# Block 1 of a two-block model kernel: the matrix memory's keys scaled, and its values placed, by ScalarE's evictions instead of by VectorE

## The chip, the cores and the metric

The kernel runs on one core of one Trainium2 chip. The metric is the device time of one execution in microseconds (us), as the median of several runs. Inputs lie in HBM in float32; the program is one launch.

## The reference, cut to what matters

The program is two blocks one after the other, each of two layers. The change lies in the first block ("block 1"), which takes 256 tokens `x` and 256 context tokens `ctx` of width 1024. Each of its layers normalizes and modulates them, projects them to 3,344 columns, and runs three mixers on pieces of the projection: a gated MLP (a), an attention (b) and a matrix memory, mLSTM, in chunks of 128 tokens (c).

```python
(au, av, az, bq, bk, bv, bz, cq, ck, cv, co, cz, cg) = _split_proj(xn @ w_in)
...
qf = qc.astype(jnp.float32)
kf = kc.astype(jnp.float32) * (D ** -0.5)          # D = 64: the factor 0.125
vf = vc.astype(jnp.float32)
...
C_new = decay[..., None, None] * C + jnp.einsum('blh,blhd,blhe->bhde', wk, vf, kf)
n_new = decay[..., None] * n + jnp.einsum('blh,blhe->bhe', wk, kf)
...
s = jnp.einsum('bthd,bshd->btsh', qf, kf) * jnp.exp(dmat - m_t[:, :, None])
num = jnp.einsum('btsh,bshd->bthd', s, vf) + inter[..., None] * jnp.einsum('bhde,bthe->bthd', C, qf)
den = jnp.sum(s, axis=2) + inter * jnp.einsum('bhe,bthe->bth', n, qf)
```

So the keys `ck` are used only times 0.125, in products with the queries and with the weighted values. The values `cv` are used with a column of ones beside them, which gives the denominators in the same products.

## The kernel before, in words

All five engines run streams of their own, written out by hand, and are tied together by semaphores. The four tiles of 128 tokens are t = 0, 1 (context) and t = 2, 3 (latent). The projection is stored in `P` (128 partitions x 4 tiles x 3,344 columns); the names AU to CG on line 35 are the columns where its pieces begin (CK = 2304, CV = 2560, CO = 2816, BZ = 1536).

The projection is made in seven chunks of columns (`CHUNKS`, line 51), in this order; below they are "chunk 0" to "chunk 6". Chunk 4 is 2048 to 2560, the memory's queries and keys. Chunk 5 is 2560 to 3072, its values and its output gate. Chunk 6 is 1536 to 2048. In the second layer (l = 1) the context tiles need less: of chunk 4 only the keys, of chunk 5 only the values, of chunk 6 nothing (`CTX_LAST`, line 53).

- TensorE. In layer 0 `project_split` (L2532) takes each of the eight blocks k of the contracted width against all four tiles, with three matmuls for each tile (lines 2546 to 2548, of high and low parts that GpSimd makes on lines 1527 and 1536). A tile has its own PSUM bank 0 to 3, and the first matmul of a tile in a chunk waits until ScalarE has emptied that bank of the chunk before (L2544). In layer 1 `project` (L2522, matmuls on L2528) makes one tile after another, in banks taken in turn; a unit waits for the eviction of four units earlier. Between the chunks TensorE does small products for the modulation vectors (L2464 and L2477 in layer 0, L2452 in layer 1).
- ScalarE. It evicts each unit from PSUM to `P` with one activation (function `evict`, L1680 to L1684), counted on the semaphore `evict`, and after each chunk does that chunk's part of `post` (L1709): after chunk 5 a tanh of the gate columns, which waits in `from_dve` for VectorE's signal `d2a` (semaphore), since VectorE's stream decides when the scratch `E` is free.
- VectorE. In `block1` (L2217) it waits until a chunk's evictions are counted, then runs `post` (L2078). After chunk 5 that is lines 2092 to 2096: scale the keys of all four tiles by 0.125 in place, copy each tile's values from `P` to `VX`, set the column of ones beside them, and `silu_part` (L1983), whose memset (L1985) is the signal `d2a` and which then waits for the tanh and makes the sigmoid of it in place (L1852). Every instruction waits for the one before it (`link`). In layer 1 it also multiplies and adds modulation weights from the ring of DMA buffers (`ada_ops`, lines 1889 and 1891), a chunk of them after the post of chunk 5.
- `VX` has 4 tiles x 4 heads x 65 columns: 64 of values and a one. It is read by GpSimd (L1551, values times weights) and by TensorE (L2702), both after the last chunk. The scaled keys are read by TensorE: transposed (L2759) and in the products of line 2710. The columns of `P` that held the values are later scratch for a tanh (L1805).

All elementwise helpers of VectorE share their lines: `tt` is L1849, `ts` is L1852 or L1853.

Of the kernel before, what the change touches and what calls it, by code (L numbers as in the profile page):

```python
# [19 lines left out]
ACT = mybir.ActivationFunctionType  # L20
# [14 lines left out]
AU, AV, AZ, BQ, BK, BV, BZ, CQ, CK, CV, CO, CZ, CG = 0, 256, 512, 768, 1280, 1408, 1536, 2048, 2304, 2560, 2816, 3072, 3328  # L35
# [97 lines left out]
def build(nc, A, out):  # L133

    es = ExitStack()
    with es:
        def sb(name, cols, rows=128):
            return es.enter_context(nc.sbuf_tensor(name, [rows, cols], F32))[:, :]
# [9 lines left out]
        P = Pf.rearrange("p (t d) -> p t d", t=T)  # L148
# [46 lines left out]
        VX = sb("VX", 16 * 65).rearrange("p (t h n) -> p t h n", t=4, h=4)  # L195
# [15 lines left out]
        def bank(b, lo=0, hi=512):  # L211
            return ps[:, b * 512 + lo:b * 512 + hi]
# [33 lines left out]
        def S(name):  # L246
            if name not in sem:
                sem[name] = es.enter_context(nc.semaphore(name))
            return sem[name]
# [1231 lines left out]
        def mlstm_units(l):  # L1481

            return [(j, d) for j in range(4) for d in range(2) if j >= 2 or l == 0]
# [73 lines left out]
        def _(act):  # L1557
            c = Count()
            s_ = nc.scalar
# [5 lines left out]
            def b128(ap):  # L1565
                return ap.partition_broadcast(128)
# [73 lines left out]
            def norm(tiles, scale, shift, mods=0, dst=None):  # L1640

                normalized_rows(tiles)
                if mods:
                    act.wait_ge(S("mods_done"), mods)
                transposed_rows(tiles, scale, shift, dst)
# [15 lines left out]
            def first_layer_rows(scale, shift):  # L1661

                def high(k):
                    act.wait_ge(S("xt_act" if k % 2 == 0 else "xt_dve"), k // 2 + 1)
                    s_.activation(XH[:, k], XT[:, k], ACT.Copy).then_inc(S("xt_hi"), 1)

                first_rows()
                act.wait_ge(S("mods_done"), 1)
                transposed_block(0, range(T), scale, shift)
                transposed_block(2, range(T), scale, shift)  # L1670
                act.wait_ge(S("hk_out"), 16)
                high(0)
                high(1)
                for k in (2, 4, 6):
                    if k + 2 < KB:
                        transposed_block(k + 2, range(T), scale, shift)
                    high(k)
                    high(k + 1)

            def evict(dst, src):  # L1680

                u = c.up("evict") - 1
                act.wait_ge(S("proj"), u + 1)
                s_.activation(dst, src(bank(u % 4)), ACT.Copy).then_inc(S("evict"), 1)  # L1684

            def from_dve():
                act.wait_ge(S("d2a"), c.up("d2a"))

# [3 lines left out]
            def rstd_small(dst, src, n):  # L1692

                from_dve()
                s_.activation(dst, src, ACT.Sqrt, scale=1.0 / n, bias=eps).then_inc(S("a2d"), 1)
# [13 lines left out]
            def post(l, ci, L):  # L1709
                if ci == 0:  # L1710

                    from_dve()
                    link(s_.activation(BB[:, 0:32], BB[:, 0:32], ACT.Exp, scale=-1.0))
                    s_.activation(BB[:, 0:32], BB[:, 0:32], ACT.Ln, bias=ones[:, 0:1]).then_inc(S("a2d"), 1)
                    silu_part(CZ, CZ + 256, L, Ef)
                elif ci == 2:
                    rstd_small(hr, hs, HD)
                elif ci == 3:
                    silu_part(AZ, AZ + 256, L, Ef)
                    for t in range(0, len(L), 2):  # L1720
                        gelu_part(L[t:t + 2])
                elif ci == 4:
                    rstd_small(lnv, lnv, HD)
                elif ci == 5:
                    silu_part(CO, CO + 256, L, Ef)
# [53 lines left out]
            def block1(l):  # L1779
                L = list(range(T)) if l == 0 else list(LAT)  # L1780
                if l == 0:
                    act.wait_ge(S("const_in"), 16)
                if l == 0:
                    first_layer_rows(lambda s: A1[:, 0, s, :], lambda s: M1[:, 0, s, 0:8])
                else:
                    norm(range(T), lambda s: A1[:, l, s, :], lambda s: M1[:, l, s, 0:8], mods=l + 1)
                for k, (lo, hi) in enumerate(CHUNKS):
                    for t in range(T):
                        rng = (lo, hi) if (t >= 2 or l == 0) else CTX_LAST[k]
                        if rng:  # L1790
                            evict(P[:, t, rng[0]:rng[1]], lambda b, r=rng: b[:, 0:r[1] - r[0]])
                    if k < 6:
                        post(l, k, L)

                for a in range(4):
                    evict(QT[:, a, L[0] * 128:512], lambda b: b[:, L[0] * 128:512])
                for a in range(2):
                    evict(KT[:, a, :], lambda b: b)
                for m in (MQT, MKT):
                    for a in range(2):  # L1800
                        evict(m[:, a, L[0] * 128:512], lambda b: b[:, L[0] * 128:512])

                act.wait_ge(S("evict"), c.at("evict"))
                for half, w in enumerate((CQ, CV)):
                    s_.activation(P[:, L[0]:T, w:w + 256], P[:, L[0]:T, BZ + 256 * half:BZ + 256 * half + 256],  # L1805
                                  ACT.Tanh, scale=0.5).then_inc(S("bz_tanh"), 1)

                attention_block1(l, [(q, h) for q in range(8) if q % 4 >= 2 or l == 0 for h in range(4)])
                for n in range(len(mlstm_units(l))):
                    act.wait_ge(S("z_T"), 8 * l + n + 1)  # L1810
                    if n >= 2:
                        act.wait_ge(S("num"), 8 * l + n - 1)
                    s_.activation(E[:, n % 2, 0:512], bank(4 + n % 2), ACT.Copy).then_inc(S("z_T_sb"), 1)
                if l == 1:
                    act.dma_start(GF, b128(A["g_final"])).then_inc(S("gf_in"), 16)
                rstd_small(hs[:, 0:16], hs[:, 0:16], HD)
                gate_rows_out(2 if l == 0 else 1)
                for kb in (0, 1, 6, 7):
                    evict(XT[:, kb, L[0] * 128:512], lambda b: b[:, L[0] * 128:512])

            def gate_rows_out(n):
                for s in range(n):
                    act.wait_ge(S("gate_rows"), c.up("gate_rows"))
                    s_.activation(GR[:, s, :], ps[:, 2048 + 1024 * s:3072 + 1024 * s], ACT.Copy
                                  ).then_inc(S("gate_rows_sb"), 1)

            block1(0)
            block1(1)

            twice_normalized_rows()  # L1830
# [4 lines left out]
        def _(dve):  # L1835
            c = Count()
            v = nc.vector

            def link(ins):
                ins.then_inc(S("chain_dve"), 1)  # L1840
                dve.wait_ge(S("chain_dve"), c.up("chain_dve"))
# [9 lines left out]
            def ts(out_, a, s1, s2=None, op0=ALU.mult, op1=ALU.add):  # L1851
                return v.tensor_scalar(out_, a, s1, s2, op0, op1) if s2 is not None else \  # L1852
                    v.tensor_scalar(out_, a, s1, None, op0)  # L1853
# [224 lines left out]
            def post(l, ci, L):  # L2078
                if ci == 0:
                    gates(l)  # L2080
                    silu_part(CZ, CZ + 256, L, Ef)
                elif ci == 2:
                    qk_norm(l)
                elif ci == 3:
                    silu_part(AZ, AZ + 256, L, Ef)
                    for t in range(0, len(L), 2):
                        gelu_part(L[t:t + 2])
                elif ci == 4:
                    layer_norm_v(L)
                elif ci == 5:  # L2090

                    link(ts(P[:, :, CK:CV], P[:, :, CK:CV], 0.125))
                    for t in range(T):
                        link(v.tensor_copy(VX[:, t, :, 0:64], P[:, t, CV:CO].rearrange("p (h d) -> p h d", h=4)))
                        link(v.memset(VX[:, t, :, 64:65], 1.0))
                    silu_part(CO, CO + 256, L, Ef, sigmoid=True)

# [312 lines left out]
            for g in range(3):  # L2410
                dve.wait_ge(S("hk_ps"), g + 1)
                hi, lo = (Qf[0:48, (3 * a + g) * HANKEL:(3 * a + g + 1) * HANKEL] for a in range(2))
# [474 lines left out]
```

## Time and profile before

| | us |
|---|---|
| median of 3 runs | 1719.9 |
| lowest and highest of the 3 | 1708.89, 1721.32 |
| the profiled execution, device time | 1723.63 |
| its span, first to last instruction | 1721.8 |
| TensorE (PE) busy in it | 1559.4 (91%) |
| VectorE (DVE) busy | 1006.2 (58%) |
| ScalarE (ACT) busy | 682.6 (40%) |
| GpSimd (POOL) busy | 171.9 (10%) |

Times in rows are us from the start of the span. "L1684" is line 1684 of the kernel; "ps" is PSUM. A row of a timeline gives start, length, engine, line, operation, what is written and what is read, and in brackets how long the engine had been idle and which instruction ended the wait. Block 1's layer 0 projects from 50 to 215 us, layer 1 from 365 to 550 us.

### The profile page before, as it was taken

How to read it: one execution, taken by the hardware profiler on the slowest of the kernel's cores; microseconds unless marked ns; L12 is line 12 of the kernel's file. 1: busy time of each engine (PE TensorE's matmuls, PEld its weight loads, DVE VectorE, ACT ScalarE, POOL GpSimd, SP SyncE). 2: the span in 40 equal slices, each digit the busy share in tenths (PEclk: the TensorE clock that was granted, in tenths of full speed). 3: DMA queues.
4: the chain of work that ended last, by engine and by line, in shares of the span. 5: the costliest groups of instructions: out<-in, count | busy, mean ns of one | idle time of the engine just before them, and what ended most of it. 6: DMA issues, size and time to landing. Idle time of an engine off the chain costs nothing.

```text
span 1721.8 us, 19030 instructions
## 1 busy us (share of the span) xinstructions
PE 1559.4 (91%) x7325; PEld 1144.0 (66%) x7325; DVE 1006.2 (58%) x1575; ACT 682.6 (40%) x1083; POOL 171.9 (10%) x194
## 2 busy tenths in 40 slices
PE   5999977888999687999989998979999898979998
PEld 2777852655655363887778877557887776567886
DVE  2348365733384653776477755457776463257776
ACT  3302137212122423563036611136664665246663
POOL 1657520000000102000110010000000000000000
PEclk8999988889999768999899988989999898989999
DMA  9656502002567213775566653059886340068882
GB/s 343 214 164 243 176 20 97 28 1 98 181 224 258 70 61 113 217 256 173 147 185 232 226 151 111 0 183 305 294 296 219 122 147 1 0 208 290 300 302 98
DMA packets 186471, 290.70 MB, mean 169 GB/s; under 512 B 13739, under 2 KB 95115, under 8 KB 186380
## 3 DMA queue, kind: packets, MB, share of 16 engines
q1 hardware_dynamic: 172080, 273.56, 46.6%
q0 software_dynamic: 13200, 13.03, 3.4%
q10 hardware_dynamic: 1100, 2.89, 0.5%
q8 instruction: 58, 0.95, 0.2%
q14 instruction: 33, 0.27, 0.0%
HBM read 287.96 MB, written 1.49 MB: 168 GB/s over the span
## 4 chain that ended last, share of the span: by engine, by line
PE 78%; DVE 12%; ACT 5%; DMA 2%; issue 2%; SPq 1%; DVEq 0%; ACTq 0%
PE ps L1127 33%; PE ps L2528 15%; PE ps L2436 3%; PE ps L2546 2%; PE ps L2547 2%; PE ps L2548 2%; PE ps L1309 2%; DVE small L2104 2%; DMA ring<-in_w_ada 2%; DVE P L1849 2%; PE ps L1290 1%; PE ps L1298 1%; DVE acc L1007 1%; ACT ps L1741 1%; PE ps L2598 1%
## 5 line engine op out<-in xcount | busy, mean ns | idle before, releaser
L1127 PE MATMUL ps<-WB,YP 128*128 128x512 f32 x1152 | 275.5, 399 | 4.7 <-DVE WB L1849 4.7
L1127 PEld LDWEIGHTS ps<-WB,YP 128*128 128x128 f32 x1152 | 218.0, 191 | 54.5 <-issue 3.8
L1849 DVE TENSOR_TENSOR WP<-ring,WP 128x2048 fp32r<-128x2048 f32 x96 | 218.8, 2290 | 50.1 <-ACT WP L694 49.8
L1127 PE MATMUL ps<-WP,XP 128*128 128x512 f32 x960 | 233.2, 396 | 9.5 <-DVE WP L1849 9.5
L1127 PEld LDWEIGHTS ps<-WP,XP 128*128 128x128 f32 x960 | 178.8, 189 | 47.2 <-DVE WP L1849 10.6
L694 ACT ACTIVATE WP<-ring 128x2048 fp32r<-128x2048 f32 x96 | 183.3, 1914 | 38.1 <-PE ps L1127 38.1
L1849 DVE TENSOR_TENSOR WB<-ring,WB 128x512 fp32r<-128x512 f32 x192 | 127.9, 690 | 86.5 <-ACT WB L611 84.6
L2528 PE MATMUL ps<-ring,XT 128*128 128x512 f32 (+3 forms) x448 | 168.4, 533 | 4.5 <-ACT XT L1657 3.3
L2528 PEld LDWEIGHTS ps<-ring,XT 128*128 128x128 f32 x448 | 88.0, 206 | 75.9 <-issue 65.9
L611 ACT ACTIVATE WB<-ring 128x512 fp32r<-128x512 f32 x192 | 114.1, 627 | 56.8 <-PE ps L1127 56.8
L1891 DVE SCALAR_TENSOR_TENSOR acc<-ring,silu_c,acc 128x512 f32<-128x512 f32 x168 | 126.0, 750 | 4.5
L1127 PE MATMUL ps<-WP,HP 128*128 128x512 f32 x480 | 115.6, 393 | 4.2 <-DVE HP L1849 4.2
L2104 DVE TENSOR_REDUCE small<-ps 128x2 f32<-128x256 f32 (+2 forms) x84 | 60.3, 717 | 81.5 <-PE ps L1323 57.8
L1127 PEld LDWEIGHTS ps<-WP,HP 128*128 128x128 f32 x480 | 90.8, 189 | 23.5 <-DVE WP L1849 4.6
L1684 ACT ACTIVATE P<-ps 128x512 f32<-128x512 f32 (+3 forms) x66 | 35.2, 545 | 174.9 <-PE ps L2548 89.5
L2546 PE MATMUL ps<-WH,XH 128*128 128x512 f32 (+1 forms) x224 | 85.4, 381 | 1.9 <-DVE XL L1849 1.9
L2547 PE MATMUL ps<-WL,XH 128*128 128x512 f32 (+1 forms) x224 | 84.7, 378 | 0.0
L2548 PE MATMUL ps<-WH,XL 128*128 128x512 f32 (+1 forms) x224 | 84.6, 378 | 0.0
L1849 DVE TENSOR_TENSOR E<-ps,GR 128x512 f32<-128x512 f32 x20 | 13.8, 692 | 115.0 <-PE ps L2528 115.0
L664 ACT ACTIVATE E<-ps 128x768 f32<-128x768 f32 x24 | 19.5, 811 | 148.6 <-PE ps L1302 148.6
L1536 POOL TENSOR_TENSOR WL<-ring,WH 128x512 fp32r<-128x512 f32 (+1 forms) x56 | 76.5, 1367 | 0.0
L2436 PE MATMUL ps<-K,P 128*128 128x128 f32 x224 | 38.6, 331 | 27.7 <-ACT P L1620 10.3
(346 smaller groups left out, 2233.3 us busy)
## 6 DMA issues: line engine op xcount, KB each, us to landing
ring<-in_w_ada SPq DMA_DIRECT2D x72, 1024.0 KB, 7.7
ring<-in_a_w_in SPq DMA_DIRECT2D x36, 1024.0 KB, 5.2
ring<-in_w_gate SPq DMA_DIRECT2D x64, 512.0 KB, 4.8
ring<-in_w_up SPq DMA_DIRECT2D x64, 512.0 KB, 6.0
ring<-in_w_down SPq DMA_DIRECT2D x32, 1024.0 KB, 7.0
ring<-in_w_in SPq DMA_DIRECT2D x24, 1024.0 KB, 9.7
ring<-in_b_w_in SPq DMA_DIRECT2D x12, 1024.0 KB, 5.2
ring<-in_w_out SPq DMA_DIRECT2D x8, 1024.0 KB, 5.2
```

What stands on the lines that cost most here:

```text
L611: s_.activation(block_slot(q)[:, 0], w, ACT.Copy).then_inc(S("b_hi"), 1)
L694: s_.activation(WP[:, (m + 1) % CONV, 0], slot(first + m), ACT.Copy).then_inc(S("w_hi"), 1)
L1127: ins = mm(dst, x(a), w(b), start=(start and n == 0), stop=(stop_ and n == 2))
L1536: nc.gpsimd.tensor_tensor(lo, w, hi.bitcast(F32), ALU.subtract).then_inc(S("win_lo"), 1)
L1849: return v.tensor_tensor(out_, a, b, op)
L1891: ins = v.scalar_tensor_tensor(o, w[:, kk, :], sc, o, ALU.mult, ALU.add)
L2104: ins = v.tensor_reduce(o[n], src, AX.X, ALU.max, negate=True)
L2436: return nc.tensor.transpose(o, i, ident[0:n, 0:n])
L2528: ins = mm(b[:, 0:hi - lo], lhs(half * kk + k, t), w[:, k, lo:hi], start=(half == 0 and k == 0), stop=(half == len(its) - 1 and k == kk - 1))
L2546: mm(b, XH[:, k, cols], hi, start=(k == 0), stop=False)
L2547: mm(b, XH[:, k, cols], lo, start=False, stop=False)
L2548: ins = mm(b, XL[:, k, cols], hi, start=False, stop=(k == KB - 1))
```

## The change

ScalarE gets two new eviction functions. `evict_keys` (chunk 4) moves the queries, where the unit has them, with one activation, and the keys with another, whose scale is 0.125. `evict_values` (chunk 5) moves the output gate, where the unit has it, with one activation, and writes the values with another straight into `VX`. Both signal `evict` once, from their last activation. VectorE's scaling of the keys and its four copies of values are gone in both layers; its four memsets of the ones stay.

```diff
+            def evict_keys(t, lo):
+
+                u = c.up("evict") - 1
+                act.wait_ge(S("proj"), u + 1)
+                if lo < CK:
+                    s_.activation(P[:, t, lo:CK], bank(u % 4, 0, CK - lo), ACT.Copy)
+                s_.activation(P[:, t, CK:CV], bank(u % 4, CK - lo, CV - lo), ACT.Copy, scale=0.125).then_inc(S("evict"), 1)
+
+            def evict_values(t, hi):
+
+                u = c.up("evict") - 1
+                act.wait_ge(S("proj"), u + 1)
+                if hi > CO:
+                    s_.activation(P[:, t, CO:hi], bank(u % 4, CO - CV, hi - CV), ACT.Copy)
+                s_.activation(VX[:, t, :, 0:64], bank(u % 4, 0, 256).rearrange("p (h d) -> p h d", h=4), ACT.Copy
+                              ).then_inc(S("evict"), 1)
...
                         rng = (lo, hi) if (t >= 2 or l == 0) else CTX_LAST[k]
-                        if rng:
+                        if rng and k == 4:
+                            evict_keys(t, rng[0])
+                        elif rng and k == 5:
+                            evict_values(t, rng[1])
+                        elif rng:
                             evict(P[:, t, rng[0]:rng[1]], lambda b, r=rng: b[:, 0:r[1] - r[0]])
...
                 elif ci == 5:
 
-                    link(ts(P[:, :, CK:CV], P[:, :, CK:CV], 0.125))
                     for t in range(T):
-                        link(v.tensor_copy(VX[:, t, :, 0:64], P[:, t, CV:CO].rearrange("p (h d) -> p h d", h=4)))
                         link(v.memset(VX[:, t, :, 64:65], 1.0))
                     silu_part(CO, CO + 256, L, Ef, sigmoid=True)
```

ScalarE's queue in layer 0, from the eviction of chunk 4 to that of chunk 6, before (the wait is on TensorE's `proj`; "x4" are the four tiles):

```order
L1684 ACTIVATE P<-ps 128x512 [waits proj] x4
L1695 ACT_TABLE_LOAD
L1695 ACTIVATE small<-small,K 128x16 [waits d2a]
L1684 ACTIVATE P<-ps 128x512 [waits proj] x4
L1690 ACT_TABLE_LOAD
L1690 ACTIVATE E<-P 128x1024 [waits d2a]
L1684 ACTIVATE P<-ps 128x512 [waits proj] x4
```

The same place with the change, from the last unit of chunk 4 on (line numbers after the new functions are larger: 1695 is now 1712, 1690 is 1707):

```order
L1691 ACTIVATE P<-ps 128x256 [waits proj]
L1692 ACTIVATE P<-ps 128x256
L1712 ACT_TABLE_LOAD
L1712 ACTIVATE small<-small,K 128x16 [waits d2a]
L1699 ACTIVATE P<-ps 128x256 [waits proj]
L1700 ACTIVATE VX<-ps 128x4x64
L1699 ACTIVATE P<-ps 128x256 [waits proj]
L1700 ACTIVATE VX<-ps 128x4x64
```

Each unit of chunks 4 and 5 is two activations there, of which the first waits. In layer 1 only the latent tiles' units are; the context tiles' stay one activation each. That makes 8 more activations in layer 0 and 4 more in layer 1.

VectorE's queue in layer 1, before, from the sum of modulation columns (M) that precedes the post of chunk 5 to the signal for the tanh:

```order
L1849 TENSOR_TENSOR M<-ps,VD 128x4 [waits ada_cols,dve_freed]
L1853 TENSOR_SCALAR P<-P 128x4x256 [waits evict,chain_dve]
L2094 COPY VX<-P 128x4x64 [waits chain_dve]
L2095 MEMSET VX 128x4 [waits chain_dve]
L2094 COPY VX<-P 128x4x64 [waits chain_dve]
L2095 MEMSET VX 128x4 [waits chain_dve]
L2094 COPY VX<-P 128x4x64 [waits chain_dve]
L2095 MEMSET VX 128x4 [waits chain_dve]
L2094 COPY VX<-P 128x4x64 [waits chain_dve]
L2095 MEMSET VX 128x4 [waits chain_dve]
L1985 MEMSET small 128x1 [waits chain_dve]
```

And with the change, to the next weights of the modulation (acc):

```order
L1870 TENSOR_TENSOR M<-ps,VD 128x4 [waits ada_cols,dve_freed]
L2114 MEMSET VX 128x4 [waits evict,chain_dve]
L2114 MEMSET VX 128x4 [waits chain_dve] x3
L2006 MEMSET small 128x1 [waits chain_dve]
L1873 TENSOR_SCALAR P<-E 128x2x256 [waits a2d,d2a]
L1910 TENSOR_SCALAR acc<-ring,silu_c 128x512 [waits slot_full_2,chain_dve]
```

Five instructions have left VectorE's queue; the wait for the evictions now stands on the first memset. Layer 0 has the same five gone. TensorE's, GpSimd's and SyncE's queues have the same instructions in the same order.

## Rows read from the trace of the kernel before

**Rows 1.** The page: busy time by engine, and the chain's shares.
```profile
PE 1559.4 (91%) x7325; PEld 1144.0 (66%) x7325; DVE 1006.2 (58%) x1575; ACT 682.6 (40%) x1083; POOL 171.9 (10%) x194
...
PE 78%; DVE 12%; ACT 5%; DMA 2%; issue 2%; SPq 1%; DVEq 0%; ACTq 0%
```

**Rows 2.** Chain that ended last, 530 to 556 us (start, us, what).
```profile
529.62 5.15 PE ps L2528 x12
534.77 0.79 PE ps L2452 x8
535.56 13.84 PE ps L2528 x32
549.40 1.69 PE ps L2452 x16
```

**Rows 3.** Timeline of VectorE, layer 0, 190 to 218 us.
```profile
192.05 0.69 DVE L1853 TENSOR_SCALAR P<-P 128x1024 f32<-128x1024 f32 x1
192.78 0.30 DVE L2094 COPY VX<-P 128x256 f32<-128x256 f32 x1
193.15 0.06 DVE L2095 MEMSET VX<- 128x4 f32 x1
193.24 0.29 DVE L2094 COPY VX<-P 128x256 f32<-128x256 f32 x1
...
194.16 0.47 DVE L2094 COPY VX<-P 128x256 f32<-128x256 f32 x1
194.71 0.06 DVE L2095 MEMSET VX<- 128x4 f32 x1
194.83 0.06 DVE L1985 MEMSET small<- 128x1 f32 x1
196.09 0.69 DVE L1852 TENSOR_SCALAR P<-E 128x1024 f32<-128x1024 f32 x1 [1.20 <-ACT E L1690]
214.59 0.24 DVE L1849 TENSOR_TENSOR M<-ps,VB 128x8 f32<-128x8 f32 x2 [17.81 <-PE ps L2477]
```

**Rows 4.** Timeline, layer 1, 534 to 541 us, the engines' rows of chunk 5's end.
```profile
534.81 0.60 ACT L1684 ACTIVATE P<-ps 128x512 f32<-128x512 f32 x1 [6.27 <-PE ps L2528]
...
535.86 0.69 DVE L1853 TENSOR_SCALAR P<-P 128x1024 f32<-128x1024 f32 x1
...
538.55 0.63 ACT L1690 ACTIVATE E<-P 128x512 f32<-128x512 f32 x1 [1.84 <-DVE small L1985]
539.29 0.43 DVE L1852 TENSOR_SCALAR P<-E 128x512 f32<-128x512 f32 x1 [0.77 <-ACT E L1690]
...
539.98 0.49 DVE L1889 TENSOR_SCALAR acc<-ring,silu_c 128x512 f32<-128x512 f32 x1 [0.27 <-DMA ring<-in_w_ada]
```

**Rows 5.** VectorE at the end of layer 1's chunk 6, 549 to 553 us.
```profile
550.29 0.16 DVE L1849 TENSOR_TENSOR M<-ps,VD 128x4 f32<-128x4 f32 x1 [4.31 <-PE ps L2452]
```

**Rows 6.** Timeline of ScalarE: evictions of 512 and of 256 columns.
```profile
162.70 2.04 ACT L1684 ACTIVATE P<-ps 128x512 f32<-128x512 f32 x4
188.06 0.60 ACT L1684 ACTIVATE P<-ps 128x512 f32<-128x512 f32 x1 [10.86 <-PE ps L2548]
520.83 0.36 ACT L1684 ACTIVATE P<-ps 128x256 f32<-128x256 f32 x1
520.83 0.64 ACT L1684 ACTIVATE P<-ps 128x256 f32<-128x256 f32 x2
```

**Rows 7.** Timeline of TensorE at the two chunk boundaries of layer 0.
```profile
168.01 0.50 PE L2546 MATMUL ps<-WH,XH 128*128 128x512 f32 x1
...
189.91 0.95 PE L2477 MATMUL ps<-K,acc 128*128 128x2 f32 x8
190.71 0.49 PE L2546 MATMUL ps<-WH,XH 128*128 128x512 f32 x1
...
192.89 0.39 PE L2546 MATMUL ps<-WH,XH 128*128 128x512 f32 x1
```

**Rows 8.** TensorE's waits, 50 to 215 us (total us, times, longest), all of them.
```profile
PE ps L2464 <- DMA ring<-in_w_ada: 2.8, 2, 1.6
```

**Rows 9.** Stretches: PE, PEld, DVE, ACT, POOL busy (count), granted clock, DMA share, GB/s.
```profile
180.00:195.00 15.00, 15.00 (x72) 12.53 (x71) 5.07 (x15) 3.75 (x6) 9.95 (x12) 1.00 1.01 362
520.00:540.00 20.00, 20.00 (x56) 9.82 (x55) 10.18 (x26) 3.96 (x7) 0.00 (x0) 1.00 0.50 180
600.00:660.00 60.00, 52.87 (x279) 34.96 (x276) 28.52 (x68) 13.83 (x27) 0.00 (x0) 0.72 0.17 55
```

## The prediction, made before the changed kernel was run

> **What bounds the kernel now.** I read the page's first part, then the chain of waits, and then the timelines of the two places that the change touches. The page says TensorE: busy for 1559.4 of 1721.8 us, and 78% of the chain, with VectorE at 12% and ScalarE at 5% [rows 1]. A share over the whole span settles nothing for one stage, so the question is what the chain is made of around the end of chunk 5, in each layer. In layer 1 the chain through the chunk-5-to-6 boundary is TensorE alone: 5.15 us of projection, 0.79 of modulation columns, 13.84 of the projection of chunk 6, 1.69 of columns, without a gap [rows 2]. In layer 0 the list of TensorE's waits from 50 to 215 us has a single row, 2.8 us for a DMA of modulation weights, and neither ScalarE nor VectorE stands in it [rows 8]. Both stretches show TensorE busy all the time, 15.00 of 15 and 20.00 of 20 us, at a granted clock of 1.00 [rows 9]. So both engines that the change touches run beside a full TensorE there. The reader should look for the covers on both sides: what VectorE waits for after the work that goes, and how long a PSUM bank may stay full before TensorE wants it.
>
> **What is removed from VectorE.** In layer 0 the scale starts at 192.05 and the next instruction at 192.78, so it takes 0.73 us with its gap. A copy takes 0.37 (192.78 to 193.15), and the last one 0.55 (194.16 to 194.71); between memset and copy lie 0.09 (193.15 to 193.24) [rows 3]. One scale and four copies: 0.73 + 3 x 0.37 + 0.55 = 2.39 us. In layer 1 I take 0.73 + 4 x 0.37 = 2.21. Together 4.60 us leave VectorE's queue.
>
> What is late next? In layer 0 the signal for the tanh, now at 194.83, comes at about 192.4, and the sigmoid, now at 196.09, follows about 2.4 us earlier. Behind it VectorE stands idle for 17.81 us until TensorE's columns of chunk 6 come [rows 3]. That idle time becomes 20.2 us, and the instruction at 214.59 starts when it did. Worth on the path: 0. ScalarE has the tanh earlier too, but its next eviction waits for TensorE's chunk 6, which no signal of VectorE starts. What a cover is worth can be said as well: without the 17.81 us, the 2.39 us would count whole.
>
> In layer 1 the tanh now starts 1.84 us late, waiting for VectorE, and ScalarE needs that time only in part: a table load stands between the last eviction and the tanh and ends just before that wait begins (538.55 - 1.84 = 536.71) [rows 4]. VectorE's signal would come 2.2 us earlier, at about 536.25, so the table load is the last to end and the tanh gains the 1.84 us minus little: I take 1.8. The sigmoid then runs at 537.5 instead of 539.29. The next instruction, the first of the modulation's weights, waits already 0.27 us for its DMA and begins at 539.98 [rows 4]. The DMA was issued when TensorE had freed the ring's slots, not by VectorE, so it lands when it did. The wait of 0.27 grows to about 2.1, and that work begins and ends as before. Even if the DMA were earlier, VectorE waits 4.31 us for TensorE at the end of it, at 550.29 [rows 5]. Worth on the path: 0, behind two covers. No transfer moves, since no slot is released earlier.
>
> **What is added to ScalarE.** 8 activations in layer 0 and 4 in layer 1, since a unit of 512 columns becomes two of 256. Four evictions of 512 columns back to back take 2.04 us; with the last one's 0.60 taken off, one starts every 0.48. Two of 256 columns take 0.64 together and 0.36 alone, so the second starts 0.28 after the first [rows 6]. A split unit therefore costs 0.56 of ScalarE's time instead of 0.48: 0.08 us more, 12 x 0.08 = 1.0 us in all. The end of a unit's eviction moves from 0.60 to 0.64 after its start.
>
> The scale of 0.125 in an eviction has no row of its own here, and neither has a write of four pieces of 64 columns, 65 apart, by ScalarE. Below, I take them as no dearer than the plain 0.28; a gain is excluded, because as many elements are read and written. Above, the nearest rows are VectorE's copies into the same `VX`, of which the slowest took 0.47 where the others took 0.29 [rows 3], so 0.47 for such an activation, and 0.28 + 0.47 = 0.75 us for a unit. The value I take is 0.56, since three of the four VX copies show no price for the pieces. The upper end would make ScalarE's extra time 12 x 0.27 = 3.2 us, and I keep it for the range.
>
> At this point a rule speaks against the change. Two activations of 256 columns against one of 512 showed 0.08 us more [rows 6]. The Trainium skill (ScalarE: Activation LUTs, What ACT_TABLE_LOAD costs) states that an activation with immediate scale and bias takes 186 ns and 0.833 ns for each element, and that successive ones overlap by about 93 ns. By that rule the split costs 186 - 93 = 93 ns a unit, an estimate of 1.1 us in all where the rows give 1.0. Either is ScalarE's time and not yet the path's.
>
> What hides it? At the end of layer 0's chunk 5 the first eviction starts at 188.06 [rows 6]. TensorE comes back to the first tile's bank at 190.71 and, nine matmuls later, to the fourth tile's at 192.89 [rows 7]. Four units of length p, one behind the other, must end by then: 188.06 + 4p < 192.89, so p may be 1.2 us before TensorE waits. My value is 0.56 and my upper end 0.75. At the end of chunk 4 ScalarE comes late, at 162.70, held up by the gelu's tanh, but TensorE spends its time on modulation rows and returns only at 168.01 [rows 6, 7]. Four units may then take 5.3 us and take 2.3 to 3.0. VectorE too waits for these evictions. After the last unit of chunk 5 in layer 1 it would be released at 534.81 + 0.64 = 535.45, or 535.7 at the upper end, and it begins at 535.86 today [rows 4]. In layer 1 TensorE needs a bank only four units later, and a unit takes it 6.9 us (0.60 of eviction and 6.27 of idle in one row [rows 4]). So the 1.0 us costs 0 on the path, and so does its upper bound of 3.2.
>
> **The sum.** Own time of the profiled execution 1723.63 - 0 (VectorE, layer 0) - 0 (layer 1) + 0 (ScalarE) = 1723.6. That execution lies 3.7 us above the median of the runs shown, 1719.9. On the scale of medians the forecast is 1719.9, which I round to 1720.
>
> **The rivals.**
>
> *The 4.60 us come off the path.* For it: ScalarE does wait for VectorE's signal, 1.84 us in layer 1 [rows 4], and every instruction of VectorE there is in a chain. Against it: the 17.81 us and the 4.31 us of idle time right behind, both ended by TensorE [rows 3, 5]. For TensorE to gain it would have to wait for VectorE somewhere in these chunks, and it doesn't [rows 2, 8]. Time: 1719.9 - 4.6 = 1715.3.
>
> *TensorE waits for banks (slower).* The place is the handover from chunk 5 to chunk 6 in layer 0, where four evictions into `VX` and `P` come one behind the other. It decides from 1.2 us a unit, twice my value. For it: an unknown access pattern, and an eviction that now ends later in the very gap in which nothing but 0.95 us of small products separates the chunks [rows 7]. Against it: the margin. If the second activation of each of the 12 units cost its full 0.37 us (0.36 alone, in rows 6) on the path, that is 12 x 0.37 = 4.4 us: 1724.3.
>
> *The time is set by which pace TensorE is granted.* The stretch from 600 to 660 us has a mean granted clock of 0.72, a mixture of full speed and half speed, that is 2.4 and 1.2 GHz, where the chunks have 1.00 [rows 9]. The three runs of the same program lie 12.4 us apart (1708.89 to 1721.32). If a later start of an idle stretch changed what is granted afterwards, the time could go to the low end, 1708.9, or as far up, to about 1731. For it: the spread is larger than every term above. Against it: TensorE's own stream keeps its starts, so nothing makes its clock differ, and three of the four times before lie from 1719.9 to 1723.6.
>
> That the change does not do what it says is not open: the order shows the five instructions gone from VectorE in both layers.
>
> **How the numbers follow.** Forecast of no change: 0.76. VectorE's time gained: 0.05. TensorE held up at banks: 0.06. Another pace, either way: 0.13, of which two thirds go down, where one of the three runs already lies. The range reaches to 1707, just under the lowest run, and to 1727, which holds the bank rival at 1724.3 with a few us of scatter between executions. All named cases lie within 1% of 1719.9, which is 17.2 us and about what a measurement of this kernel can tell from no change. Only a small part of the last two leaves it: faster by over 1% 0.04, within 1% 0.91, slower by over 1% 0.05.
>
> **What would show the steps right or wrong.** In the changed profile VectorE's idle time before the columns of layer 0's chunk 6 should be about 20.2 us instead of 17.81, and in layer 1 the wait for the modulation's DMA about 2.1 instead of 0.27, with 4.31 at the end unchanged. The tanh after layer 1's chunk 5 should follow its table load at once. ScalarE should have 12 more activations of about 0.37 us, and the pairs should be 0.28 apart. TensorE's waits up to 215 us should still be the DMA alone. I am wrong if a wait of TensorE for ScalarE's evictions appears there, if a write into `VX` takes over 0.9 us, or if the chunks from 530 to 550 us come earlier by a microsecond or two relative to their layer's start.

## The result, and the profile after

The changed kernel takes 1725.6 us (median of 20 runs, 1710.3 to 1729.6) beside 1720.2 for the kernel before (20 runs, 1703.9 to 1724.5). The ratio is 1.0048, with an interval of 1.0025 to 1.0071. So it is slower, by about 5 us by the medians and 8 by the ratio: less than 1%, inside the range of the forecast, and not the forecast of no change. Comparisons leave disturbed runs out.

The profiled execution doesn't show this loss. It has a device time of 1721.8 us and a span of 1719.9, at a mean granted clock of 0.927, where the one of before had 1723.6, 1721.8 and 0.918. (The span is the time from the first to the last instruction; the granted clock is the share of full speed that TensorE was given.) One execution scatters more than the change moves, so what follows compares places, not whole spans.

The page, as in [rows 1]:

```profile
PE 1556.0 (90%) x7325; PEld 1140.3 (66%) x7325; DVE 1002.6 (58%) x1565; ACT 683.4 (40%) x1095; POOL 173.6 (10%) x194
...
PE 78%; DVE 13%; ACT 5%; DMA 2%; issue 2%; SPq 1%; DVEq 0%; ACTq 0%
```

VectorE has 10 instructions fewer and 3.6 us less work, ScalarE 12 more and 0.8 us more work.

Timeline of VectorE, layer 0, the place of [rows 3] (start, duration, engine, line, instruction, in brackets the idle time before it and what ended it):

```profile
192.77 0.46 DVE L2114 MEMSET VX<- 128x4 f32 x4
193.29 0.06 DVE L2006 MEMSET small<- 128x1 f32 x1
194.55 0.69 DVE L1873 TENSOR_SCALAR P<-E 128x1024 f32<-128x1024 f32 x1 [1.20 <-ACT E L1707]
215.28 0.24 DVE L1870 TENSOR_TENSOR M<-ps,VB 128x8 f32<-128x8 f32 x2 [20.03 <-PE ps L2496]
```

The idle time before the columns of chunk 6 grew from 17.81 to 20.03 us. The 2.2 us that were saved became waiting. (The whole stretch lies 0.7 us later here, from its first row to its last.)

Timeline of VectorE in layer 1, the place of [rows 4, 5]:

```profile
535.66 0.46 DVE L2114 MEMSET VX<- 128x4 f32 x4
536.19 0.06 DVE L2006 MEMSET small<- 128x1 f32 x1
537.28 0.43 DVE L1873 TENSOR_SCALAR P<-E 128x512 f32<-128x512 f32 x1 [1.03 <-ACT E L1707]
539.90 0.49 DVE L1910 TENSOR_SCALAR acc<-ring,silu_c 128x512 f32<-128x512 f32 x1 [2.20 <-DMA ring<-in_w_ada]
550.06 0.16 DVE L1870 TENSOR_TENSOR M<-ps,VD 128x4 f32<-128x4 f32 x1 [4.15 <-PE ps L2471]
```

Here the wait for the DMA took the time over, 2.20 us where it was 0.27, and behind it the wait for TensorE is 4.15 where it was 4.31.

Timeline of ScalarE: the split evictions of chunk 4 (first two rows) and chunk 5 in layer 0, then the tanh of layer 1 [rows 4, 6]:

```profile
163.43 0.37 ACT L1691 ACTIVATE P<-ps 128x256 f32<-128x256 f32 x1
163.70 0.38 ACT L1692 ACTIVATE P<-ps 128x256 f32<-128x256 f32 x1
163.96 0.39 ACT L1691 ACTIVATE P<-ps 128x256 f32<-128x256 f32 x1
...
188.74 0.38 ACT L1699 ACTIVATE P<-ps 128x256 f32<-128x256 f32 x1 [10.80 <-PE ps L2567]
189.03 0.38 ACT L1700 ACTIVATE VX<-ps 128x256 f32<-128x256 f32 x1
189.42 0.39 ACT L1699 ACTIVATE P<-ps 128x256 f32<-128x256 f32 x1
...
190.78 0.38 ACT L1699 ACTIVATE P<-ps 128x256 f32<-128x256 f32 x1
...
535.25 1.28 ACT L1707 ACT_TABLE_LOAD   x1
536.54 0.63 ACT L1707 ACTIVATE E<-P 128x512 f32<-128x512 f32 x1
```

A unit of chunk 4, with the scale in it, takes 0.53 us (163.43 to 163.96), a unit of chunk 5 0.68 (188.74 to 190.78, three units). The tanh follows its table load at once.

All of TensorE's waits from 50 to 216 us [rows 8]:

```profile
PE ps L2483 <- DMA ring<-in_w_ada: 2.7, 2, 1.6
```

The DMA stands there alone, so TensorE waits for no bank. It is also as busy as before at the chunks (columns as in [rows 9]):

```profile
180.00:195.00 15.00, 15.00 (x72) 12.52 (x71) 4.11 (x12) 4.99 (x10) 9.94 (x11) 1.00 0.97 348
520.00:540.00 20.00, 20.00 (x56) 9.64 (x55) 8.21 (x20) 4.08 (x9) 0.00 (x0) 1.00 0.51 179
```

So far everything is as it was forecast, and the kernel is slower. What is new stands behind both places. These are VectorE's waits that were ended by VectorE itself (total us, times, longest), all of them:

```profile
DVE small L2123 <- DVE small L1874: 0.2, 1, 0.2
DVE X L1874 <- DVE small L2233: 0.2, 1, 0.2
```

The profile of before has no such row. Each is an instruction that starts some 0.2 us after the last one of its own engine has ended, with no other wait in the profile. Below they are called pauses. The chain of waits goes through the first of the two, before the row maxima of layer 1's attention (changed kernel):

```profile
580.04 0.19 DVE small L1874
580.23 0.24 issue
580.47 1.24 DVE small L2123
```

and the same step of the kernel before:

```profile
578.81 0.19 DVE small L1853
579.00 0.02 issue
579.03 1.24 DVE small L2104
```

"issue" is 0.24 us where it was 0.02. That time is on the path. The second pause, before the scaling of a tile of X at the end of layer 1, seems to be covered, as VectorE then waits 1.25 us for TensorE:

```profile
670.46 0.75 DVE L1874 TENSOR_SCALAR X<-P,small 128x1024 f32<-128x1024 f32 x1 [0.21 <-DVE small L2233]
672.47 0.69 DVE L1870 TENSOR_TENSOR E<-ps,GR 128x512 f32<-128x512 f32 x1 [1.25 <-PE ps L2547]
```

### The profile page after: what moved, and what is told of

It is laid out like the page before. It is cut to its first block, busy times and chain, and to the rows that moved or that the text cites. A ratio compares the mean times of both kernels' runs of the same rounds, so it can differ in the third digit from the quotient of the medians.

```text
span 1719.9 us, 19032 instructions
## 1 busy us (share of the span) xinstructions
PE 1556.0 (90%) x7325; PEld 1140.3 (66%) x7325; DVE 1002.6 (58%) x1565; ACT 683.4 (40%) x1095; POOL 173.6 (10%) x194
## 4 chain that ended last, share of the span: by engine, by line
PE 78%; DVE 13%; ACT 5%; DMA 2%; issue 2%; SPq 1%; DVEq 0%; ACTq 0%
PE ps L1127 33%; PE ps L2547 15%; PE ps L2455 3%; PE ps L2565 2%; PE ps L2567 2%; PE ps L2566 2%; PE ps L1309 2%; DVE small L2123 2%; DMA ring<-in_w_ada 2%; DVE P L1870 2%; PE ps L1290 1%; ACT ps L1758 1%; PE ps L1298 1%; DVE acc L1007 1%; PE ps L2483 1%
## 5 line engine op out<-in xcount | busy, mean ns | idle before, releaser
L1684 ACT ACTIVATE P<-ps 128x512 f32<-128x512 f32 (+3 forms) x50 | 27.3, 547 | 147.6 <-PE ps L2567 78.8
```

## The experiments

Each was run five rounds against the kernel before; ratios have their 95% interval. "Pauses" are rows in which VectorE's idle time was ended by VectorE's own instruction, read from the one profile of each kernel. A pause that falls into a wait for another engine has no such row, so the count is a lower bound.

**Which half of the change?** Keys alone (values copied and written as before) and values alone (keys scaled by VectorE as before):

```
keys only:    if rng and k == 4: evict_keys(t, rng[0])      and no  link(ts(P[:, :, CK:CV], ..., 0.125))
values only:  if rng and k == 5: evict_values(t, rng[1])    and no  link(v.tensor_copy(VX[:, t, :, 0:64], ...))
```

> The keys' half of the change alone: ScalarE's chunk-4 evictions are split and scale by 0.125, VectorE's scale is gone, the values are evicted and copied as before. Theory 'split' (the two-part evictions cost the time, through something the profile's waits don't show): 6 of the 12 extra activations, so about +2.5 to +4 us over before. Theory 'release' (VectorE's earlier release of the tanh and of what follows costs it): 1.46 of the 4.6 us go, so +1 to +2.5 us. Theory 'pace' (any shift of covered work changes in which stretches TensorE is granted half speed, with no part owning the loss): anything from -3 to +6 us, with the stretches at a granted clock of 1.00 equal to before's within 0.5 us, and a time that goes with the mean granted clock.

> The values' half alone: ScalarE's chunk-5 evictions are split and write VX, VectorE's copies are gone, its scale of the keys stays. Theory 'split': the other 6 extra activations, +2.5 to +4 us. Theory 'release': 3.1 of the 4.6 us go, +3 to +5 us. Theory 'pace': anything from -3 to +6 us, not tied to the sum of the two halves (the halves need not add up to the whole's +5.5).

Keys only: 1.0017 [0.9987, 1.0047], no pause. Values only: 0.9994 [0.9963, 1.0025], one pause, at another place. Neither half shows the loss, though the intervals reach up to 1.0047 and 1.0025. Each holds its own half of ScalarE's split evictions.

**Is it ScalarE's part or VectorE's?** The changed kernel with VectorE's instructions put back as idle work of the same shapes (a scale by 1.0 and a copy of VX onto itself):

```
                 elif ci == 5:
+                    link(ts(P[:, :, CK:CV], P[:, :, CK:CV], 1.0))
                     for t in range(T):
+                        link(v.tensor_copy(VX[:, t, :, 0:64], VX[:, t, :, 0:64]))
                         link(v.memset(VX[:, t, :, 64:65], 1.0))
```

> The changed kernel with VectorE's time put back: it multiplies the keys by 1.0 and copies VX onto itself, in the places of the work that went, so that the tanh comes as late as before, while ScalarE's evictions stay split. Theory 'split': as slow as the changed kernel, +4 to +8 us over before. Theory 'release': as before, within 1.5 us. Theory 'pace': no forecast of the sign; within -3 to +6 us.

1.0006 [0.997, 1.0042], no pause. With all of ScalarE's part and VectorE's queue at its old length, no loss is seen.

The kernel before with the scale and the copies after the sigmoid's part, so that ScalarE gets its signal early and nothing is removed:

```
-                    link(ts(P[:, :, CK:CV], P[:, :, CK:CV], 0.125))     (and the copies)
                     silu_part(CO, CO + 256, L, Ef, sigmoid=True)
+                    link(ts(P[:, :, CK:CV], P[:, :, CK:CV], 0.125))
+                    for t in range(T):
+                        link(v.tensor_copy(VX[:, t, :, 0:64], P[:, t, CV:CO].rearrange("p (h d) -> p h d", h=4)))
```

> The kernel before with VectorE's scale and copies moved behind the sigmoid of chunk 5: the signal for the tanh comes about 2.4 us earlier as in the changed kernel, ScalarE's evictions are not split, and all the work is still done, in time in which VectorE was idle. Theory 'split': as before, within 1.5 us. Theory 'release': +4 to +8 us like the changed kernel. Theory 'pace': no forecast of the sign; within -3 to +6 us. By the waits in the profile alone: 0.

1.001 [0.9977, 1.0042], no pause. The early signal isn't it either.

**Is the loss there again, and what does nothing give?** Both kernels unchanged, and the kernel before with 12 activations of one column added behind the evictions:

```
+                            if k in (4, 5) and rng == (lo, hi):
+                                s_.activation(idle[:, 8 * l + 4 * (k - 4) + t:...], eps, ACT.Copy)
```

> The changed kernel itself, on a chip and at a time at which its halves are as fast as the kernel before. Theory 'interaction' (the two halves together cost what neither costs alone): +5 to +8 us over before again, as in the first comparison. Theory 'pace' (the first comparison's difference came from which stretches were granted half speed): within 3 us of before here, or a difference that goes with the mean granted clock at about 1.1 us for each 0.001.

> The kernel before, unchanged, as if it were a changed one. It bounds what a comparison of a dozen runs with the pooled runs of before can tell. Both theories: 0, within 3 us; if it lies further off, such distances say nothing of an edit.

> The kernel before with 12 extra activations of one column each on ScalarE, behind the evictions of the same 12 units of chunks 4 and 5; they write scratch that nobody reads, and no other instruction moves. They lengthen ScalarE's queue there by about 1 to 2 us, as the splits do. Theory 'split' or 'interaction': extra activations behind full units cost +2 to +5 us by themselves. Theory 'pace': within 3 us of before, with the same stretches as before at a granted clock of 1.00.

The changed kernel again 1.0044 [1.0008, 1.008], with the same two pauses; the kernel before against itself 1.0009 [0.9972, 1.0046], none; 12 more instructions on ScalarE alone 1.0034 [0.9995, 1.0072], none. The loss repeats, and it isn't noise. The third value leaves a part of it possible through ScalarE's queue, which only the filled and the padded kernel (below) argue against.

**Is the time lost within block 1?** Both kernels with block 2 left out (so they stop after block 1, and the program's result isn't computed):

> Block 1 of the kernel before alone: the program ends after its last layer's output is normalized, block 2 and its weights are left out (so its time, near 660 us, stands against e9 and not against before). It is the reference for e9. Both theories: no forecast but the scatter, which theory 'pace' puts at 2 to 5 us between executions also here.

> Block 1 of the changed kernel alone, block 2 left out as in e8. Theory 'interaction' (the change costs block 1 some us by itself): +4 to +8 us over e8, all of it in block 1. Theory 'pace': the change's own stage costs nothing, so within 1.5 us of e8, or a difference that its granted clock shows; what the whole kernel loses would then arise in block 2, whose code is the same, by where its stretches meet the steps of the clock.

698.6 us (688.0 to 704.8, all 5 runs) without the change, 691.2 (682.2 to 697.2, all 6 runs) with it, though the changed one has its two pauses. About 660 us had been expected for either. Block 1 alone isn't slower. The scatter is wider than the effect, and the program is another one, so this says no more than that nothing of 5 us shows there.

**Does it hang on the moment at which block 2 is reached?** Twelve chained memsets on VectorE before the final scaling (1.4 us in both profiles, where 1.1 had been estimated); 1 or 19 extra matmuls of 128 columns in block 2's first projection (19 take 4.4 us in both profiles, where 3.2 had been estimated):

```
+                    for _ in range(12):
+                        link(v.memset(gtmp[:, 0:1], 0.0))
```
```
+                    if item_kind == "awin" and first == 0 and n == 2:
+                        for _ in range(19):
+                            mm(bank(us[0] % 4, 0, 128), ident, ident, start=True, stop=True)
```

> The changed kernel with 12 chained one-column memsets on VectorE (about 1.1 us) on the path between block 1 and block 2, nothing else. Theory 'interaction': 1 us slower than the changed kernel, so +6.5 to +9 us over before. Theory 'pace': block 2 meets the clock's steps elsewhere, so the time can fall in spite of more work: anywhere from -2 to +8 us over before, not the changed kernel plus 1.

> The kernel before with the same 12 memsets (about 1.1 us) on the path between the blocks. Theory 'interaction' and plain addition: +1 us. Theory 'pace': anywhere from -3 to +7 us; the distance of e10 to e11 is not the +5.5 us of the changed kernel over before.

> The changed kernel with 19 more matmuls of 128 columns (0.171 us each, 3.2 us in all) on TensorE inside block 2's first projection, into a bank that the next matmul overwrites. Theory 'interaction' (the change itself costs the 6 us): the changed kernel plus 3, so about +9 us over before. Theory 'pace' (the change pushes block 2 onto the course with more half speed beside its attention): the shift puts it on the short course, which is worth about 10 us, so -3 to +2 us against before, faster than the changed kernel in spite of more work.

> The kernel before with one such matmul (0.17 us) in the same place. Theory 'interaction' or plain addition: +0.2 us, nothing that can be seen. Theory 'pace': it moves block 2 by a little more than the 0.1 us that separates the short courses from the long ones in the profiles, so more executions take the long one: +4 to +9 us.

> The changed kernel with one such matmul. It is mostly on the long course already, so both theories: the changed kernel's time, +5 to +8 us over before.

> The kernel before with the 19 matmuls, 3.2 us. Theory 'interaction' or plain addition: +3 us. Theory 'pace': also about +3 us or a little less, since most of its executions are on the short course and stay there, and the rest come over to it; what tells is e12 minus e15, which is 0 to 2 us by 'pace' and 6 us by 'interaction'.

| edit | on the changed kernel | on the kernel before |
|---|---|---|
| 12 memsets | 1.0034 [1.0003, 1.0065] | 0.999 [0.9958, 1.0021] |
| 1 matmul | 1.0038 [1.0008, 1.0068] | 1.0016 [0.9986, 1.0045] |
| 19 matmuls | 1.0059 [1.003, 1.0088] | 1.0053 [1.0019, 1.0086] |

My theory at that time was that a slightly later start of block 2 changes the pace TensorE is granted there. A start that is merely later doesn't do it: 1.4 us of delay on the kernel before cost nothing that can be seen, one matmul on it gave no clear loss where 4 to 9 us were expected, and 19 matmuls on the changed kernel made it about 10 us slower than before, by the ratio, where -3 to +2 were expected. One row speaks for such an effect: 4.4 us of matmuls cost the kernel before about 9 us, and with them the two kernels are 1 us apart. That a change of pace in block 2 does hold the loss, whatever sets it off, is read from the profiles in the last section.

**Does it hang on the length of VectorE's queue?** The changed kernel with five one-column memsets a layer, which brings VectorE back to 1575 instructions; the kernel before made 10 instructions shorter by one memset for all tiles and one copy (three in layer 1) for several; and the changed kernel made 6 shorter still:

```
padded:        + for _ in range(5): link(v.memset(gtmp[:, 0:1], 0.0))      (after the sigmoid's part)
shortened:     + link(v.memset(VX[:, :, :, 64:65], 1.0))
               + for t0, t1 in ((0, 4),) if l == 0 else ((0, 2), (2, 3), (3, 4)):
               +     link(v.tensor_copy(VX[:, t0:t1, :, 0:64], P[:, t0:t1, CV:CO]...))
one memset:    + link(v.memset(VX[:, :, :, 64:65], 1.0))                   (for the changed kernel's four)
```

> The changed kernel with five one-column memsets on VectorE behind the sigmoid of chunk 5 in each layer, in idle time: VectorE executes as many instructions as in the kernel before, and releases the tanh as early as in the changed one. Theory 'queue length' (ten instructions fewer move VectorE's own short pauses onto the path before block 2, and block 2 then takes the course with more half speed): the two pauses are gone from the profile, and the time is that of before, within 3 us. Theory 'evictions' (ScalarE's split evictions or the early release cause it in some other way): as slow as the changed kernel, +5 to +8 us.

> The kernel before with the same scaling, copies and ones made by fewer VectorE instructions: one memset for all tiles, and one copy in layer 0 and three in layer 1 in place of four, so six fewer in layer 0 and four in layer 1, ten in all as in the changed kernel; ScalarE is as before. Theory 'queue length': the two pauses of 0.25 us appear in layer 1, and the time is +4 to +8 us over before. Theory 'evictions': as before, within 3 us, or a little faster.

> The changed kernel with one memset of the ones for all four tiles in place of four, in both layers: sixteen VectorE instructions fewer than before instead of ten. Theory 'queue length': the pauses lie elsewhere, and the time is decided by whether they are again on the path into block 2; if the profile has none there, within 3 us of before. Theory 'evictions': as slow as the changed kernel, +5 to +8 us.

The padded one takes 1718.2 us, 0.9986 [0.9954, 1.0019]. Its interval lies wholly under that of the changed kernel's first comparison, [1.0025, 1.0071], and overlaps the repeat's, [1.0008, 1.008], by a little. Ten instructions that do nothing take the loss away. Its chain has no pause before the row maxima:

```profile
579.14 0.19 DVE small L1874
579.34 0.02 issue
579.36 1.24 DVE small L2125
```

The shortened kernel before, which has none of the change, shows both pauses, at the same two instructions (its waits of VectorE for itself):

```profile
DVE small L2104 <- DVE small L1853: 0.2, 1, 0.2
DVE X L1853 <- DVE small L2214: 0.2, 1, 0.2
```

It takes 1.0024 [0.9995, 1.0054]: the direction that was looked for, in an interval that still touches no change. With 16 instructions fewer there is one pause, elsewhere, and 1.0029 [0.9999, 1.006]:

```profile
DVE small L1870 <- DVE small L2267: 0.2, 1, 0.2
```

No version beats the kernel before clearly.

**All runs side by side, at an equal clock.** The time of an execution goes with its mean granted clock. One straight line through 348 executions, 141 of them of the kernel before (one slope, a level for each kernel), falls 1.08 us for each 0.001 of clock. The levels at a clock of 0.9235, with errors of 0.7 to 1.0 us for the versions and 0.3 for the kernel before, are worked out from the results' times and clocks, and the grouping was made after the runs:

| pauses in the profile | kernels | level, us |
|---|---|---|
| none | before 1719.4, again 1719.8, keys only 1717.3, filled 1720.1, later 1720.4, null edit 1719.0, memsets 1719.0, 1 matmul 1720.6, padded 1718.3 | 1717.3 to 1720.6 |
| one | values only 1719.4, changed with memsets 1721.1, changed with one memset 1721.4 | 1719.4 to 1721.4 |
| two | changed 1723.4, again 1724.0, with 1 matmul 1723.2, before shortened 1722.3 | 1722.3 to 1724.0 |
| with 4.4 us of matmuls | before (none) 1726.1, changed (two) 1726.1 | 1726.1 |

Of the changed kernel's distance, then, the mean clock carries some 3 us (0.9224 on average beside 0.9250 in the 141), and 4.0 us stay at an equal clock (4.6 in the repeat). The padded kernel lies 5.1 us under the changed one. The levels go with the number of pauses, but for the last row and with an overlap of the first two. That is a correlation: every kernel with two pauses is the changed one or the shortened one.

## Why the prediction was right and wrong

- *VectorE's removed work is worth 0, layer 0.* Right: idle time 20.2 forecast, 20.03 found.
- *Layer 1.* Right: the DMA's wait 2.1 forecast, 2.20 found, the tanh starts behind its table load, and 4.15 us of waiting for TensorE are left at the end.
- *ScalarE's units.* 0.56 us was forecast for each. Those with the scale took 0.53, those into VX 0.68: no price of the scale is seen, and behind the activation into pieces (0.38 itself) the next one starts 0.39 later, against 0.29 in a pair. Both are under the upper end of 0.75. Against the 0.48 of an unsplit unit the splits cost 0.05 and 0.20. The estimate of 93 ns a split, worked out from what the Trainium skill (ScalarE: Activation LUTs, What ACT_TABLE_LOAD costs) states, lies between the two. All of it stays hidden, as said.
- *The rival of 4.60 us off the path* and *the rival of banks* both fell: the waits named above, and TensorE's list without ScalarE.
- *The sum, "Own time of the profiled execution 1723.63 - 0 - 0 + 0 + 0".* This is the step that failed. Its terms count what instructions take, wait for and hide, and each came out near 0 as said. No term was for VectorE's queue being ten instructions shorter, whatever these were, and the measured loss is 5 us by the medians. That the ten instructions decide it is shown by the padded kernel (1718.2 us, 0.9986 beside the changed one's 1.0048), and the filled one points the same way; the shortened one, at 1.0024, leans that way without being clear; that it moves pauses of VectorE to two fixed instructions is shown by the changed kernel twice and the shortened one once.
- *The pace rival's "TensorE's own stream keeps its starts, so nothing makes its clock differ".* This failed too. A start on the path moved, if only by 0.2 us, and in the profiles TensorE runs block 2, whose code is the same, at another pace (last section). So a change of pace, which had 0.13, is the rival that the profiles come nearest to, though its direction was wrong: it was to go down in two of three cases, and the time went up.
- *The range, up to 1727.* That it holds 1725.6 is luck: its upper end was made for the rival of banks, which didn't happen.

What stays open is how ten instructions do it. In the profiles the pauses put 0.24 us on the path, and TensorE's idle time in the span is 163.9 us in the changed kernel (1719.9 - 1556.0) and 162.4 in the one before, with 166.1 in the second profile of the one before. So the missing 4 to 5 us are not waiting time of TensorE. They can lie in the pace of its work, and the last section shows that block 2's differs. That the pauses are what leads there is not shown. What a pause is, the supply of instructions to the engine for example, no row names, and no run tried it.

## What to carry to other kernels

When work is taken off an engine that waits anyway, the time can still move by half a per cent, as here, with the number of instructions that stay in its queue. So before an effect of that size is explained by the work, put as many cheap instructions back as were removed and measure that. And look in the waits for rows in which an engine was released by itself: they cost little each, but they show a delay that no wait in the profile accounts for. When one profile of each kernel doesn't show the loss, cut each at a place that all share, here the start of block 2, and compare the parts.

## What the runs showed that was not expected

The pauses themselves: 0.18 to 0.29 us, where the usual gap between VectorE's instructions in the chain is 0.02. They stand at the same two instructions in both profiles of the changed kernel, at another one with 2 instructions more (values only), and at yet another with 6 fewer (one memset).

The same program has more than one course through block 2. Here is one stretch of it in two profiles of the unchanged kernel before (columns as in [rows 9]), first:

```profile
805.00:890.00 85.00, 76.11 (x468) 61.85 (x467) 49.02 (x79) 11.81 (x16) 16.78 (x24) 0.84 0.54 141
```

and in the second profile:

```profile
805.00:890.00 85.00, 76.22 (x498) 62.40 (x499) 54.77 (x85) 15.23 (x22) 16.79 (x24) 0.94 0.64 164
```

The clock is 0.84 and 0.94, with TensorE as busy in both, and 30 more matmuls done in the second; the spans are 1721.8 and 1707.6 us. The padded kernel, as fast as the one before, was profiled on the first course:

```profile
805.00:890.00 85.00, 76.11 (x469) 61.88 (x468) 49.05 (x79) 11.81 (x16) 16.78 (x24) 0.84 0.56 142
```

So the course of one profiled execution doesn't tell a kernel's median, and spans of single profiles can't be compared below 1%.

The courses can be told apart, though, when each profile is cut at the first matmul of block 2's first projection. Here is block 2 alone, from there to the end of the span, in the changed kernel, then in the first and in the second profile of the kernel before:

```profile
690.40:1719.90 1029.50, 961.34 (x4623) 755.84 (x4623) 653.18 (x919) 479.80 (x696) 29.10 (x44) 0.94 0.57 187
689.00:1721.80 1032.80, 964.92 (x4623) 758.99 (x4623) 652.86 (x919) 479.91 (x696) 29.04 (x44) 0.93 0.57 186
688.10:1707.60 1019.50, 952.19 (x4623) 748.87 (x4623) 653.12 (x919) 480.17 (x696) 29.07 (x44) 0.95 0.58 188
```

The instructions are the same, the busy time of VectorE, ScalarE and GpSimd is equal within 0.4 us, and TensorE's differs by up to 12.7 us, with its idle time within 0.9. So what differs is the pace at which TensorE works: its granted clock is 0.94, 0.93 and 0.95. Block 2's length takes few values:

| profiles | block 2, us |
|---|---|
| two pauses: changed, again, with 1 matmul, before shortened | 1029.1 to 1029.5 |
| none or one: before again, later, filled, null edit, changed with one memset | 1019.3 to 1019.5 |
| none or one: keys only, values only, before with memsets | 1013.3 to 1013.5 |
| none or one: before, before with 1 matmul, padded, changed with memsets | 1032.8 to 1033.1 |
| with 19 matmuls, so with more work in block 2 | changed (two pauses) 1029.2, before (none) 1035.3 |

Without the last row, all four profiles with two pauses are on one course, which no other profile takes. The two short ones are taken by 8 of the 12 others. Block 2 begins no later in the four (690.0 to 699.3 us) than in the others (688.1 to 703.3). The unprofiled executions fit that: below 1716 us lie 59 of 141 of the kernel before and 5 of 11 of the padded one, but only 3 of 31 of the changed kernel and 2 of 12 of the shortened one. So the loss looks like short courses that have become rare, rather than some us added to every execution. That reading, and the bound of 1716 us, were made after the runs, with one profile a kernel; what sends an execution on one course or the other is not shown.
